# A mixture-of-experts kernel: ScalarE instead of GpSimd copies the prefetched second-layer weights

## The reference

```python
logits = xt @ router_w + router_b          # 256 tokens, 32 experts
top_v, top_e = lax.top_k(logits, 4)
gate = softmax(top_v)
for e in range(32):                        # the tokens that chose expert e
    hb = xb @ w1[e] + b1[e]                # w1[e]: 1024 x 2048
    g, u = hb[:, :1024], hb[:, 1024:]
    g = minimum(g, 7.0); u = clip(u, -7.0, 7.0)
    y = ((u + 1) * g * sigmoid(1.702 * g)) @ w2[e] + b2[e]   # w2[e]: 1024 x 1024
    out[tokens] += gate * y
```

## Time and profile before

| | |
|---|---|
| median of 3 runs | 2168.78 us (2166.72 to 2171.35) |
| profiled execution, its own time | 2165.81 us |
| its span, first to last instruction | 2163.6 us |
| mean granted clock of TensorE | 0.957 of full speed |
| PE busy | 1933.4 us, 89% |
| DVE busy | 833.4 us, 39% |
| ACT busy | 452.9 us, 21% |
| POOL busy | 222.8 us, 10%, 124 instructions |
| DMA traffic | 590.98 MB, 273 GB/s over the span |
| largest share of the chain that ended last | DMA of the experts' first-layer weights, 26% |

### The profile page before, as it was taken

One profiled execution on the slowest core, in us unless ns is written; L12 is line 12 of the kernel. 1 busy time (PEld: TensorE's weight loads), 2 busy tenths in 40 slices (PEclk: granted clock), 3 DMA queues, 4 the chain that ended last, 5 costly groups with the idle time before them and its releaser, 6 DMA issues.

```text
span 2163.6 us, 29263 instructions
## 1 busy us (share of the span) xinstructions
PE 1933.4 (89%) x10886; PEld 1107.7 (51%) x10887; DVE 833.4 (39%) x1547; ACT 452.9 (21%) x875; POOL 222.8 (10%) x124
## 2 busy tenths in 40 slices
PE   6999998987899878867777898999999999999997
PEld 3767767521233212211212222476499976648996
DVE  2223233333232331343233413224367744436776
ACT  1322231100011000000000101112345431024543
POOL 0000000012213222222222212000000000000000
PEclk9999998988999999998999999999999999999999
DMA  9244582699999999999999999933276645433652
GB/s 358 100 156 178 206 243 80 249 385 424 424 410 367 425 424 426 426 426 425 425 425 426 426 378 427 382 117 107 49 209 180 190 128 129 136 107 103 189 174 88
DMA packets 189167, 590.98 MB, mean 273 GB/s; under 512 B 10579, under 2 KB 110738, under 8 KB 153140
## 3 DMA queue, kind: packets, MB, share of 16 engines
q1 hardware_dynamic: 187084, 587.69, 71.6%
q10 hardware_dynamic: 2024, 2.46, 0.4%
HBM read 589.05 MB, written 2.63 MB: 273 GB/s over the span
## 4 chain that ended last, share of the span: by engine, by line
PE 66%; DMA 27%; DVE 3%; ACT 1%; issue 1%; SPq 0%; ACTq 0%; DVEq 0%
DMA lower<-in_exp_w 26%; PE psum L2078 12%; PE psum L1458 8%; PE psum L2090 5%; PE psum L1818 5%; PE psum L1568 5%; PE psum L1573 5%; PE psum L1827 4%; PE psum L1600 3%; PE psum L1540 2%; PE psum L1862 2%; PE psum L1546 1%; PE psum L1466 1%; PE psum L1901 1%; DMA lower<-in_mod_w 1%
## 5 line engine op out<-in xcount | busy, mean ns | idle before, releaser
L962 POOL COPY upper<-upper 128x2048 f32<-128x2048 f32 x120 | 222.6, 1896 | 1113.3 <-PE psum L1881 780.2
L1827 PE MATMUL psum<-lower,upper 128*32 128x512 f32 x1280 | 191.7, 722 | 107.1 <-DMA lower<-in_exp_w 100.7
L2078 PEld LDWEIGHTS psum<-rounded 128*128 128x128 f32 x2112 | 257.4, 188 | 3.6
L2078 PE MATMUL psum<-rounded 128*128 128x256 f32 x2112 | 258.8, 282 | 0.0
L1818 PE MATMUL psum<-lower,upper 128*64 128x512 f32 x896 | 207.3, 608 | 34.3 <-DMA lower<-in_exp_w 34.3
L2544 DVE TENSOR_SCALAR upper<-psum 128x512 f32<-128x512 f32 (+1 forms) x34 | 23.0, 678 | 521.7 <-PE psum L1827 321.4
L1458 PE MATMUL psum<-upper,lower 128*128 128x256 f32 (+1 forms) x880 | 165.6, 388 | 4.1 <-ACT upper L1008 4.1
L1827 PEld LDWEIGHTS psum<-lower,upper 128*32 128x32 f32 x1280 | 37.2, 121 | 254.6 <-issue 134.6
L1818 PEld LDWEIGHTS psum<-lower,upper 128*64 128x64 f32 x896 | 60.5, 137 | 178.5 <-issue 119.6
L1458 PEld LDWEIGHTS psum<-upper,lower 128*128 128x128 f32 (+1 forms) x880 | 130.2, 173 | 35.5 <-issue 10.8
L2531 DVE TENSOR_SCALAR upper<-lower,upper 128x32 f32<-128x32 f32 x132 | 136.6, 1104 | 0.0
(11 more groups left out here) (393 smaller groups left out, 2022.8 us busy)
## 6 DMA issues: line engine op xcount, KB each, us to landing
lower<-in_exp_w SPq DMA_DIRECT2D x128, 2048.0 KB, 24.8
upper<-in_exp_w SPq DMA_DIRECT2D x128, 1024.0 KB, 19.9
lower<-in_ffn_w_up SPq DMA_DIRECT2D x88, 512.0 KB, 5.3
lower<-in_mod_w SPq DMA_DIRECT2D x12, 2048.0 KB, 10.3
lower<-in_w_in SPq DMA_DIRECT2D x12, 2048.0 KB, 9.5
lower<-in_ffn_w_down SPq DMA_DIRECT2D x44, 512.0 KB, 5.7
lower<-in_odd_w_in SPq DMA_DIRECT2D x8, 2048.0 KB, 11.2
lower<-in_even_w_in SPq DMA_DIRECT2D x7, 2048.0 KB, 12.4
```

What stands on the lines that cost most here:

```text
L962: pool.tensor_copy(w2_pair[j], w2_ahead[j]).then_inc(w2_in[2 * j], 16)
L1827: ins = pe.matmul(o[32 * r:32 * r + 32].rearrange("p (g n) -> p g n", g=2), rows[:, 0:FEW], gate_and_up(k, r), start=first, stop=last, til ...
L2078: ins = pe.matmul(bank[4 + b][:, T * g:T * g + T], w[:, g, k, :], x[:, k, :], start=(k == m == 0), stop=(k == KD - 1 and m == 2))
```

## The change

POOL's program is removed. ACT makes the same 120 copies, as `activation` with the function Copy. They stand behind the whole work of an expert: behind its output copy, and for an expert with more than 64 tokens behind the wait for `ov["done"]`. ACT's loop over the experts is cut in two, 0 to 29 with the copies of the weights of expert e + 1, and 30 to 31 without. The waits are the old ones, and so are the semaphores that SP and PE wait for. The programs of SP, PE and DVE are unchanged.

```diff
-        @block.gpsimd
-        def _(pool):
-
-            with pool.Fori(1, N_EXP - 1) as e:
-                for j in range(KD // 2):
-                    pool.wait_ge(w2_ahead_in[j], e * 16)
-                    pool.nop(nofuse=True)
-                    pool.wait_ge(w2_used, e * KD + (2 * j + 2 - KD))
-                    pool.nop(nofuse=True)
-                    pool.tensor_copy(w2_pair[j], w2_ahead[j]).then_inc(w2_in[2 * j], 16)
-
         @block.scalar
         def _(act):
...
             copy_gathered(1)
-            with act.Fori(0, N_EXP) as e:
+            def expert(e):
                 count = act.value_load(counts_int_i[0:1, bass.ds(e, 1)], min_val=0, max_val=T)
                 with act.If(count > SLOTS):
...
                 with act.Else():
                     main_turn(e)
                     main_output(e)
+
+            def fill_second_layer(e):
+
+                for j in range(KD // 2):
+                    act.wait_ge(w2_ahead_in[j], e * 16)
+                    act.nop(nofuse=True)
+                    act.wait_ge(w2_used, e * KD + (2 * j + 2 - KD))
+                    act.activation(w2_pair[j], w2_ahead[j], ACT.Copy).then_inc(w2_in[2 * j], 16)
+
+            with act.Fori(0, N_EXP - 2) as e:
+                expert(e)
+                fill_second_layer(e + 1)
+            with act.Fori(N_EXP - 2, N_EXP) as e:
+                expert(e)
```

## The result

| | before | changed |
|---|---|---|
| median | 2168.78 us (5 runs, 2163.08 to 2171.35) | 2182.89 us (5 runs, 2176.86 to 2187.87) |
| profiled execution | 2165.81 us | 2176.86 us |
| its span | 2163.6 us | 2174.7 us |
| ratio, 95% interval | | 1.0067 (1.0042 to 1.0091) |

The changed kernel is slower, by 0.67%. The medians differ by 14.1 and 12.9 us; the forecast was 8.7.

What follows compares the result with a forecast made beforehand. DMA was taken to bound the expert stage. Late refills behind experts 6 and 27, 3.5 + 5.2 = +8.7 us net of PE's earlier start, gave 2177.5 us against the 2168.78 us median; range 2168 to 2185 us.

Steps and rivals of the forecast that it cites:

- Sign, place and mechanism: Slower by about 8.7 us, from late refills into an empty DMA queue behind experts 6 and 27; chance 0.60.
- The copy's price: One 128x2048 copy on ScalarE takes 1.9 us, four take 7.3 us.
- Ordinary experts at 0: In one-pass experts a DMA queue of some 15 us and ScalarE's idle time cover the later copies: cost 0.
- its cover of 4.9 us: Behind expert 7, 1.4 us over an empty queue plus the lag cover the refills' own 3.2 us delay.
- The start of the two experts: PE's transposes L1937 come 2.4 us earlier in expert 6 and 0.7 us earlier in expert 27.
- the stand of 1.5 us: PE waits some 1.5 us for ScalarE's copy L1218, queued behind four weight copies, when experts 6 and 27 start.
- The lower clock: If PE's stand for L1218 drops the granted clock, PE loses up to 1.7 us each time, 0 to 3.4 us.
- The end: Refills behind experts 6 and 27 start later, so the first 2048 KB pieces land 3.5 and 5.2 us late.
- Rival (a): Faster by the freed VectorE/GpSimd port at the start of experts 6 and 27: 6.7 us, 2162.1 us; chance 0.07.
- Rival (b): The DMA lag behind the two-pass experts is absorbed and nothing is measured, 2168.8 us; chance 0.18.
- Rival (c): Slower still, about 2182 us, by lower clock both times, or 2.1 us copies and a second-code cost; chance 0.15.
- the second code: The first pass through ScalarE's second loop, experts 30 and 31, was taken as 0, at most +2 us.

Runs made afterwards that it cites:

- e2: Changed kernel, but in experts of up to 64 tokens ScalarE makes three copies ahead of the output copy, the fourth behind it: ratio 1.0031, 2176.68 us.
- e4: Kernel before, GpSimd keeping the copies but starting them only behind ScalarE's output copy of the expert: ratio 1.0019, 2174.37 us.
- e6: Changed kernel, with ScalarE's copies beside the second layer in experts 6, 7, 27 and 28 only: ratio 0.9997, 2169.19 us.
- e7: Changed kernel, with the four copies ahead of the wait for ov["done"] in two-pass experts: ratio 1.0037, 2178.50 us.
- e1: Changed kernel, but in experts 6 and 27 ScalarE makes three copies ahead of the output copies, the fourth behind them: ratio 1.0039, 2178.84 us.
- e3: Changed kernel, but in every expert ScalarE makes three copies ahead of the output copy, the fourth behind it: ratio 0.9954, 2160.28 us.
- e8: Kernel before, with GpSimd's copies cut to 16 of 2048 columns, waits and DMAs kept: ratio 0.9975, 2164.13 us.
- e5_control: Changed kernel measured again, unaltered, against the kernel before: ratio 1.0058, 2182.34 us.
- e9: Kernel before, with only ScalarE's expert loop cut into 0 to 29 and 30 to 31: ratio 1.0003, 2170.19 us.

## Why the prediction was right, and where its size was off

- **Sign, place and mechanism** were right. The loss is behind experts 6 and 27, made by refills that come late into an empty queue (0 GB/s from 654 to 662 us); e2, e4, e6 and e7 show it from four sides. The size was too small: 8.7 us against 13.0 in the stage and 14.1 and 12.9 between the medians.
- **The copy's price**, 1.9 us and 7.3 us for four, was measured as 1.899 and 7.30.
- **Ordinary experts at 0**: right for the changed kernel (504.3 us against 504.6 over 17 experts, tanh always released by DVE). What was too simple was to take expert 7 as covered for good: its cover of 4.9 us was 3.5 us of lag from expert 6 and 1.4 of its own. It held in the changed kernel, where the lag was there, and fell away in e1, which took the lag out.
- **The start of the two experts**: 2.4 us was forecast and measured for L1937; the stand of 1.5 us was 1.86. The lower clock behind it, which I had put in the range and not in the sum, came in expert 6 in each of the five profiles with that stand, in expert 27 in two of five. That step took 1.7 us off the win: of its 2.4 us expert 6 kept 0.8 (L1904 starts 47.9 us after the output copy of expert 5, where L1901 started 48.7 us after it). It is the largest single step of the miss.
- **The end**: 3.5 and 5.2 us were forecast, 6.7 and 6.4 measured. Besides the clock (1.7 us, expert 6) two terms were too small, at both experts. The copies start 0.5 us behind the end of L1901 (660.51 against 658.01 + 1.99) and not 0.1: 0.4 us each. And the four refills need 8.4 us from the first landing to the last (667.4 to 675.8), not the 7.4 us of three times 2.47: 1.0 us each, together more than the clock. Why four refills that are issued 1.8 us apart land 2.8 us apart no run shows. 8.7 + 1.7 + 0.8 + 2.0 = 13.2 us, against 13.0 in the stage. The sum comes out, but it was put together from the result and is no test.
- **Rival (a)**, the freed port, was a real price but not in this kernel: ScalarE's own queue took it. e3 and e8 collect it, 7.1 and 6.9 us, near to the 6.7 us worked out for it. The rule of the Trainium skill (SBUF — State Buffer, Who interferes with whom) holds in these traces: in e3 VectorE's four selects took 0.68 us at 608.04, in the middle of ScalarE's copies, where the earlier trace rows show 6.87 us beside GpSimd's.
- **Rival (b)**, the lag absorbed, is refuted: from expert 9 to 26 nothing is won back. **Rival (c)** was nearest in time, 2182 us, and its first reason, the lower clock, came once in this profile and twice in that of e5_control. It accounts for 1.7 us of the 4.3; the second code (e9) and slower copies play no part, and the two terms above were in no rival.

## What to carry to other kernels

Where DMA is the bound, don't judge a moved copy by how idle its new engine is; look for the smallest time from issue to landing among the DMAs that wait for the copy, since only there does its moment count. Then look again with the first hole closed: the lag of one hole can be all that covers the next. An engine with 17 us of idle time per step is still the wrong one if its next urgent instruction, or a wait of its own, stands beside the copies in the same queue. Moving the same work to the same engine, but into the order in which its inputs fall free, turned +0.6% into -0.45%.

## What the runs showed of the hardware

The granted clock of TensorE falls to the lower of its levels (2.4 to 1.2 GHz) behind a stand of 1.86 us in some executions and not in others, in the same program at the same place: five times of five in expert 6 and twice of five in expert 27. In the seven profiles without that stand the 16 matmuls at this place took 3.66 us in both experts. The rows are of the windows view of the changed kernel, behind the stand in expert 6 and behind that in expert 27; the granted clock is 0.50 in the one and 1.00 in the other.

```profile
619.80:622.80 3.00, 3.00 (x10) 0.97 (x8) 0.84 (x6) 0.00 (x0) 0.00 (x0) 0.50 1.02 421
1254.80:1257.80 3.00, 3.00 (x15) 0.98 (x16) 1.35 (x6) 0.00 (x0) 0.00 (x0) 1.00 0.95 401
```

The clock scatters ahead of the copies too. The stretch from 430 to 460 us, ahead of all but the first two of the moved copies, had a mean granted clock of 0.89 in the profile of before and of 0.61 in that of e1, and the first output copy came at 460.6 and 469.4 us. Of these 8.8 us, 3.2 were there by PE's first matmuls of L1913 (432.01 and 435.25); 5.6 came behind them. First before, then e1_two_early:

```profile
430.00:460.00 30.00, 27.36 (x172) 9.78 (x171) 11.10 (x35) 2.43 (x4) 1.90 (x2) 0.89 0.85 340
```

```profile
430.00:460.00 30.00, 27.55 (x119) 9.13 (x117) 7.85 (x36) 2.11 (x4) 0.00 (x0) 0.61 0.62 235
```

So a single profile's total is good to some 9 us here, while the stretch from expert 9 to 26, in which DMA moves 424 GB/s and more in nearly every slice, is 504.2 to 505.0 us in all twelve profiles.
